# Where a routed feed-forward adds an expert's outputs back: at the end of its round, or after the second weight tile of the next round

## The reference

```python
def swiglu(h, wg, wu, wd):
    return (jax.nn.silu(h @ wg) * (h @ wu)) @ wd

def moe(h, router, wg, wu, wd):
    logits = (h @ router).astype(jnp.float32)
    vals, idx = lax.top_k(logits, TOP_K)
    w = jax.nn.softmax(vals, axis=-1)
    gates = jnp.sum(jax.nn.one_hot(idx, N_EXPERTS) * w[..., None], axis=-2)
    y = jnp.zeros_like(h)
    for e in range(N_EXPERTS):
        y = y + gates[..., e:e + 1] * swiglu(h, wg[e], wu[e], wd[e])
    return y
...
x = x + g2 * moe(h, ...)                           # D = 1024, D_FF = 3072
return rmsnorm(x, final_g)
```

## Time and profile before

| | us |
|---|---|
| median of three runs | 2789.95 |
| the profiled execution | 2787.62 |
| its span, first to last instruction | 2785.8 |
| PE busy in the span | 2625.9 |
| DVE busy | 1974.1 |
| ACT busy | 1384.5 |
| eight rounds of the routed feed-forward, about | 1889.7 to 2771.1 |

### The profile page before, as it was taken

One profiled execution on the slowest core, in us unless ns is written; L12 is line 12 of the kernel. 1 busy time (PEld: TensorE's weight loads), 2 busy tenths in 40 slices (PEclk: granted clock), 3 DMA queues, 4 the chain that ended last, 5 costly groups with the idle time before them and its releaser, 6 DMA issues. The chain is left out here.

```text
span 2785.8 us, 42232 instructions
## 1 busy us (share of the span) xinstructions
PE 2625.9 (94%) x14598; PEld 2260.7 (81%) x14598; DVE 1974.1 (71%) x2695; ACT 1384.5 (50%) x1697; POOL 0.2 (0%) x4
## 2 busy tenths in 40 slices
PE   8979878999999999999799998979999999999998
PEld 3769768887888889999687998867888888888886
DVE  6768235988777877776554653528788798898886
ACT  3454223133444444444353433427677777676775
POOL 0000000000000000000000000000000000000000
PEclk9999899999999999999999999989999999999999
DMA  6531223632678877876242553418899999998995
GB/s 243 210 114 46 69 76 123 190 112 90 226 264 291 298 281 257 282 257 228 90 166 77 182 183 123 167 61 304 321 364 333 326 373 330 358 347 322 371 333 210
DMA packets 223290, 626.83 MB, mean 225 GB/s; under 512 B 15296, under 2 KB 23520, under 8 KB 222816
## 3 DMA queue, kind: packets, MB, share of 16 engines
q1 hardware_dynamic: 223200, 625.64, 63.6%
HBM read 619.29 MB, written 6.29 MB: 225 GB/s over the span
## 5 line engine op out<-in xcount | busy, mean ns | idle before, releaser
L3133 DVE TENSOR_TENSOR wide_low<-wide,wide_high 128x2048 fp32r<-128x2048 f32 x288 | 657.1, 2286 | 125.9 <-ACT wide_high L3080 122.5
L3080 ACT ACTIVATE wide_high<-wide 128x2048 fp32r<-128x2048 f32 x288 | 550.9, 1918 | 182.7 <-DMA wide<-in_moe_gu 91.3
L229 DVE TENSOR_TENSOR expert_tile_low<-slot,expert_tile_high 128x1024 fp32r<-128x1024 f32 x216 | 263.9, 1223 | 129.9 <-ACT expert_tile_high L221 125.7
L221 ACT ACTIVATE expert_tile_high<-slot 128x1024 fp32r<-128x1024 f32 x216 | 227.3, 1054 | 189.2 <-PE bank L238 78.1
L2985 PE MATMUL bank<-wide_high,xg_high 128*128 128x512 f32 x768 | 305.4, 398 | 4.3 <-ACT wide_high L3080 4.3
L2986 PE MATMUL bank<-wide_high,xg_low 128*128 128x512 f32 x768 | 300.3, 391 | 0.0
L2989 PE MATMUL bank<-wide_low,xg_high 128*128 128x512 f32 x768 | 207.3, 392 | 0.2 <-DVE wide_low L3133 0.2
L237 PE MATMUL bank<-h_high,expert_tile_high 128*128 128x256 f32 x704 | 173.2, 284 | 0.0
L1899 PE MATMUL bank<-expert_tile_high,act_hi 128*128 128x512 f32 x512 | 161.3, 396 | 12.2 <-DVE act_lo L2040 12.2
L238 PE MATMUL bank<-h_low,expert_tile_high 128*128 128x256 f32 x704 | 172.7, 283 | 0.0
L2985 PEld LDWEIGHTS bank<-wide_high,xg_high 128*128 128x128 f32 x768 | 144.8, 189 | 33.6 <-ACT wide_high L3080 4.5
(11 more groups left out here) (500 smaller groups left out, 5084.1 us busy)
## 6 DMA issues: line engine op xcount, KB each, us to landing
wide<-in_moe_gu SPq DMA_DIRECT2D x192, 1024.0 KB, 5.8
wide<-in_moe_d SPq DMA_DIRECT2D x96, 1024.0 KB, 6.5
slot<-in_peer_u SPq DMA_DIRECT2D x128, 512.0 KB, 4.3
slot<-in_peer_v SPq DMA_DIRECT2D x128, 512.0 KB, 4.4
slot<-in_w_in SPq DMA_DIRECT2D x72, 512.0 KB, 3.4
picked_or_ada<-in_ada_w SPq DMA_DIRECT2D x48, 512.0 KB, 5.0
ada_slot<-in_ada_w SPq DMA_DIRECT2D x48, 512.0 KB, 4.6
slot<-in_ffn_gu SPq DMA_DIRECT2D x48, 512.0 KB, 3.4
```

The costliest lines, as they stand in the source:

```text
L221: core.nc.scalar.activation(self.tile_hi[:, place % 2], core.slot[u][:], ACT.Copy).then_inc(self.hi_ready.sem, 1)
L229: core.nc.vector.tensor_tensor(self.tile_lo[:, place % 2], slot[:], self.tile_hi[:, place % 2].bitcast(F32), ALU.subtract)\
L3080: nc.scalar.activation(w_hi[n % NB][:].rearrange("p c n -> p (c n)"), wide[n % U][:], ACT.Copy).then_inc(hi_ready.sem, 1)
L3133: nc.vector.tensor_tensor(w_lo[n % NB][:].rearrange("p c n -> p (c n)"), wide[n % U][:], w_hi[n % NB][:].rearrange("p c n -> p (c n)").bit ...
```

## The change

After the change the outputs are kept in banks 4 and 5 until the next round has begun. ACT copies them after its copy of tile 1, scaled by a column of shares for each place, to `y_high`; DVE makes `y_low` from the same bank behind the low part of tile 1. PE scatters behind tile 1: 16 matmuls, high and low part with `back`, which is now unscaled and F32R. The `take`s stand behind tiles 3 to 6, two each. `turn_pick` transposes `pick` with the identity and multiplies `pick` with a one-column vector of shares. The same round body now also scatters in the first round, where the banks, the column of shares and `back` are zero; after the loop one scatter follows for the last round.

```diff
-    yg = sb("yg", [P, D])
+    y_hi, y_lo = sb("y_high", [P, D], F32R), sb("y_low", [P, D], F32R)
-    back = sb("back", [P, N])
-    shared = sb("share_diagonal", [P, 2, P])
+    back = sb("back", [P, N], F32R)
+    of_tokens = sb("shares_of_tokens", [P, 2, 1])
+    of_places = sb("shares_of_places", [P, 1])
...
-    SPREAD = (6, 7, 1, 3)
+    SPREAD = (1, 3, 6, 7)
...
-            def scatter():
+            def scatter(k):
+                pe.wait_ge(backs.sem, backs.at(1) + k)
+                pe.wait_ge(x_ready.sem, x_ready.at(2) + k * 2)
                 for s in range(4):
+                    if s % 2 == 0:
+                        pe.wait_ge(y_split.sem, y_split.at(s // 2 + 1) + k * 2)
                     for j in range(2):
                         m = 2 * s + j
-                        last = nc.tensor.matmul(core.bank[SPREAD[s]][:, j * N:j * N + N], yg[:, m * P:m * P + P], back[:, :], start=True, stop=True)
+                        out = core.bank[SPREAD[s]][:, j * N:j * N + N]
+                        nc.tensor.matmul(out, y_hi[:, m * P:m * P + P], back[:, :], start=True, stop=False)
+                        last = nc.tensor.matmul(out, y_lo[:, m * P:m * P + P], back[:, :], start=False, stop=True)
                     last.then_inc(scattered.sem, 1)
...
             def turn_pick(k):
-                pe.wait_ge(diagonals.sem, diagonals.at(1) + k)
+                pe.wait_ge(columns.sem, columns.at(1) + k)
+                pe.wait_ge(y_split.sem, y_split.at(2) + k * 2)
                 for tt in range(2):
-                    last = nc.tensor.matmul(core.bank[4][:, tt * P:tt * P + P], pick[:, tt, :], shared[:, tt, :], start=True, stop=True)
+                    nc.tensor.transpose(core.bank[4][:, tt * P:tt * P + P], pick[:, tt, :], core.ident)
+                for tt in range(2):
+                    last = nc.tensor.matmul(core.bank[4][:, N:N + 1], pick[:, tt, :], of_tokens[:, tt, :], start=(tt == 0), stop=(tt == 1))
...
+                        if j == 0 and w == 0:
+                            scatter(k)
...
-                pe.wait_ge(backs.sem, backs.at(1) + k)
-                pe.wait_ge(y_kept.sem, y_kept.at(2) + k * 2)
-                pe.wait_ge(x_ready.sem, x_ready.at(4) + k * 2)
-                scatter()
+            scatter(n_rounds(pe))
...
+            def keep_outputs(k):
+                for b in range(2):
+                    if b == 0:
+                        act.wait_ge(y_made.sem, y_made.at(1) + k)
+                    else:
+                        act.wait_ge(used.sem, used.at(NB) + k * T)
+                    nc.scalar.activation(y_hi[:, 512 * b:512 * b + 512], core.bank[Y[b]][:, :], ACT.Copy, scale=of_places[:, 0:1])\
+                        .then_inc(y_kept.sem, 1)
...
+                    if n == 1:
+                        keep_outputs(k)
...
-                for b in range(2):
-                    act.wait_ge(y_made.sem, y_made.at(1) + k) if b == 0 else act.wait_ge(used.sem, used.at(NB + T) + k * T)
-                    nc.scalar.activation(yg[:, 512 * b:512 * b + 512], core.bank[Y[b]][:, :], ACT.Copy).then_inc(y_kept.sem, 1)
+            keep_outputs(n_rounds(act))
...
+            def low_outputs(k, b):
+                dve.wait_ge(y_kept.sem, y_kept.at(b + 1) + k * 2)
+                nc.vector.scalar_tensor_tensor(y_lo[:, 512 * b:512 * b + 512], core.bank[Y[b]][:, :], of_places[:, 0:1],
+                                               y_hi[:, 512 * b:512 * b + 512].bitcast(F32), ALU.mult, ALU.subtract).then_inc(y_split.sem, 1)
...
-                    if n < C:
-                        take(k, (4, 5, 6, 7, 0, 1, 2, 3)[n])
+                    if n == 1:
+                        for b in range(2):
+                            low_outputs(k, b)
+                    if 3 <= n < 7:
+                        for m in range(2 * n - 6, 2 * n - 4):
+                            take(k, m)
                     if n == C:
                         dve.wait_ge(pick_turned.sem, pick_turned.at(1) + k)
+                        nc.vector.tensor_copy(of_places[:], core.bank[4][:, N:N + 1])
                         nc.vector.tensor_copy(back[:, :], core.bank[4][:, 0:N]).then_inc(backs.sem, 1)
```

More of the change, by code:

```diff
@@ L2937, in routed_feed_forward @@
         "moe_silu", "moe_hidden", "moe_hidden_turned", "moe_hidden_high", "moe_hidden_low"))
-    picks, gathered, x_high, x_ready, backs, y_made, y_kept, scattered, added, diagonals, pick_turned = (core.count(n) for n in (
+    picks, gathered, x_high, x_ready, backs, y_made, y_kept, y_split, scattered, added, columns, pick_turned = (core.count(n) for n in (
         "picks_ready", "tokens_gathered", "gathered_high", "gathered_low", "backs_ready", "outputs_made", "outputs_kept",
-        "outputs_scattered", "outputs_added", "share_diagonals", "picks_turned"))
+        "outputs_low", "outputs_scattered", "outputs_added", "share_columns", "picks_turned"))
     J = D_FF // 512
@@ L3100, in make_pick, with take_shares @@
                 ins.then_inc(picks.sem, 1)
-            def make_diagonal(k):
+            def take_shares(k):
                 e = expert_of(dve, k)
-                for tt in range(2):
-                    ins = nc.vector.tensor_scalar(shared[:, tt, :], core.ident, shares[:, tt, bass.ds(e, 1)], None, ALU.mult)
-                ins.then_inc(diagonals.sem, 1)
+                nc.vector.tensor_copy(of_tokens[:], shares[:, :, bass.ds(e, 1)]).then_inc(columns.sem, 1)
+            def low_outputs(k, b):
+                dve.wait_ge(y_kept.sem, y_kept.at(b + 1) + k * 2)
+                nc.vector.scalar_tensor_tensor(y_lo[:, 512 * b:512 * b + 512], core.bank[Y[b]][:, :], of_places[:, 0:1],
+                                               y_hi[:, 512 * b:512 * b + 512].bitcast(F32), ALU.mult, ALU.subtract).then_inc(y_split.sem, 1)
             def low_gathered(k):
@@ L3121, in _ @@
             make_pick(0)
-            for b in (1, 3):
-                nc.vector.memset(core.bank[b][:, :], 0.0).then_inc(scattered.sem, 1)
-            make_diagonal(0)
+            nc.vector.memset(of_places[:], 0.0)
+            nc.vector.memset(core.bank[Y[1]][:, :], 0.0)
+            nc.vector.memset(core.bank[Y[0]][:, :], 0.0).then_inc(y_made.sem, 1)
+            for tt in range(2):
+                ins = nc.vector.tensor_copy(back[:, tt * P:tt * P + P], core.zeros[:].bitcast(F32))
+            ins.then_inc(backs.sem, 1)
+            take_shares(0)
             low_gathered(0)
-            for b in (6, 7):
-                dve.wait_ge(x_ready.sem, x_ready.at(2))
-                nc.vector.memset(core.bank[b][:, :], 0.0).then_inc(scattered.sem, 1)
             with dve.Fori(0, n_rounds(dve)) as k:
@@ L3134, in _ @@
                                             w_hi[n % NB][:].rearrange("p c n -> p (c n)").bitcast(F32), ALU.subtract).then_inc(lo_ready.sem, 1)
-                    if n < C:
-                        take(k, (4, 5, 6, 7, 0, 1, 2, 3)[n])
+                    if n == 1:
[4 more added lines that the diff above has]
+                            take(k, m)
                     if n == C:
                         dve.wait_ge(pick_turned.sem, pick_turned.at(1) + k)
+                        nc.vector.tensor_copy(of_places[:], core.bank[4][:, N:N + 1])
                         nc.vector.tensor_copy(back[:, :], core.bank[4][:, 0:N]).then_inc(backs.sem, 1)
                         make_pick(k + 1)
-                        make_diagonal(k + 1)
+                        take_shares(k + 1)
                     if n >= 5 and n % 4 == 1 and n < T1 + 4:
@@ L3154, in _ @@
             rounds = n_rounds(dve)
+            for b in range(2):
+                low_outputs(rounds, b)
             for m in range(C):
```

## The result

The changed kernel took 2774.09 us (median of five runs, 2771.97 to 2779.14) against 2789.62 for the kernel before (five runs): ratio 0.9941, 95% interval 0.9925 to 0.9956. Faster by 15.5 us; forecast were 14.3 us and 2775.6 us. In a second set of runs the same kernel had 0.9931 (0.9916 to 0.9947).

What follows compares the result with a forecast made beforehand. PE was taken to bound the kernel, with the weight loads near their limit. Seven turns gain 16.2 us, round 0 loses 2.3, the tail gains 0.4: 14.3 us off 2789.95 gives 2775.6 us, range 2770 to 2788.

Steps and rivals of the forecast that it cites:

- What bounds: Whole round: PE and weight loads both near their limit; PE waits only where a round ends.
- the 361 GB/s of mid-round: Load supply after the turn: at this rate a round needs 104.6 us, 2.8 less than PE's 107.4.
- The turn: PE between rounds: gap, old scatter and low-part wait go, new scatter and `turn_pick` come; net 2.3 us, seven turns 16.2.
- its slow first matmul: Tile 0's first matmul at the old turn, 0.41 us; left in place, cause unknown between scatter and loop's turn.
- the 0.08 us booked behind the new scatter: PE after the scatter: first wide matmul after small ones takes 0.31 us instead of 0.23.
- The bare turn: Rival at the round's end: loop's turn, no longer hidden behind the scatter, costs PE 3.37 us; 2799 to 2800 us; chance 0.05.
- ACT's order as cover: ACT at the turn: tiles 0 and 1 copied before the outputs, ready at -2.2 and -0.3 us from tile 0's start.
- Round 0 and the tail: First round scatters zeros, 2.3 us lost; after the last round copies and `take`s end earlier, 0.4 us gained.
- The room of `y_low`: DVE early in the round: both halves ready at 3.7 us, PE asks at 5.4; 1.7 us of room, 1.2 at worst.
- the rival of the late outputs: Rival: late tile 0 load brings output parts after 5.4 us; PE waits, 2 us a round gives 2789 us; chance 0.09.

Runs made afterwards that it cites:

- scatter_twice: Changed kernel with each pair of scatter matmuls issued twice, 32 instead of 16; a round took 108.97 us against 107.05.
- eleven_products: Changed kernel with one of the twelve matmuls of each tile left out; a round took 103.09 us against 107.05.
- plain_new_place: Changed kernel with the scatter behind tile 1 in plain 32-bit floats, without low part; round 108.57 us, ratio to the kernel before 0.9964.
- keep_first: Changed kernel with ACT's copies of the outputs ahead of its copy of tile 0 again; round 111.16 us, ratio to the kernel before 1.0042.
- split_old_place: Changed kernel with copies, low parts and F32R scatter at the end of the round; round 111.06 us, ratio to the kernel before 1.0033.
- no_zero_scatter: Changed kernel with first round written out without scatter, copies and adds, and 20 matmuls behind the last scatter; ratio to the kernel before 0.9945.
- after_tile_0: Changed kernel with the scatter behind tile 0 on PE instead of tile 1; a round took 107.44 us against 107.05.

## Why the prediction was right

- **What bounds.** PE, with the loads close behind. scatter_twice shows the first, eleven_products the second: room for 4.0 us a round, where the prediction had worked out 2.8 from the 361 GB/s of mid-round. That working was not sound. In that stretch PE was busy for 95.00 of 95.00 us, and a round of the kernel before without its turn takes PE about 104.9 us (109.69 - 4.43 - 0.38, the last two as below), which asks for 360 GB/s: the 361 was PE's own pace. What the loads could do lay only a little above it, 366 GB/s, which no row of before could show. That the conclusion held is in part luck.
- **The turn.** Forecast 4.63 us removed and 2.31 added, net 2.3. Measured 109.81 - 107.05 = 2.76 in the mean, 109.69 - 107.05 = 2.64 against the rounds of before that had no late load. The 4.43 us from tile 35 to tile 0 went whole, as forecast. The scatter was sized right (1.92, the row of the same form). Tile 0 took 3.10 us before and 2.72 now, 0.38 less, where only 0.2 was booked: the 0.18 us of its slow first matmul, left in place by the prediction, came from the plain scatter ahead of it and not from the loop's turn (plain_new_place has it behind tile 1). `turn_pick` grew by 0.22, not 0.31, and the 0.08 us booked behind the new scatter did not come: a wide matmul starts 0.23 after its predecessor there. That gives 4.43 + 0.38 - 1.92 - 0.22 = 2.67, near the 2.64.
- **The bare turn.** The loop's turn itself costs PE nothing: 2220.50 follows 2219.60 + 0.90, and this rival falls. The fetch after a taken branch to code outside the window, of which the Trainium skill speaks in "Runtime: NRT & Kernel Launch", section "Instruction fetch mechanics", is not to be seen. The instruction queues moved five packets each from 1880 to 2785 us; before it was five and four. The spacing that the Trainium skill gives in "TensorE: Matmul & The Clock Gate", section "Wait — 56ns, not 53.3ns?", would have made the scatter 1.75 us by an estimate; the new one took the 1.92 of the row.
- **Which part pays.** The prediction summed PE's terms and treated ACT's order as cover. The runs show that this cover is the condition: keep_first costs 4.1 us a round, split_old_place 4.0. The place gives 1.24, the form 1.52 on top of it; at the old place the form, with its extra step on VectorE, costs 1.25 (111.06 against 109.81).
- **Round 0 and the tail.** From the first gathered copy to the start of tile 35 of round 0 passed 111.08 us before and 113.40 now: 2.3 us lost, as forecast. From the last tile to the norm the gain was 0.4 us, as forecast: the last four matmuls started at 2764.51 before the norm at 2771.42 and now at 2754.83 before 2761.31, so 6.91 became 6.48.
- **What the sum had left out.** The stage gained 17.3 us: seven turns at 2.64, 0.7 from the late loads in two rounds of before, less 2.3 for round 0, and 0.4 at the end. The forecast was 14.3. The norm behind the stage took 1.7 us longer, since part of its matmuls ran at the lower clock; the prediction had no term for that. Stage and norm make 15.6, and the medians differ by 15.5. This near agreement isn't shown to be more than chance: the two profiled executions differ by only 8.5 us, since in the changed kernel's the stage began 7.2 us later. The prediction's closeness is partly luck as well, a turn sized 0.3 too small against a norm that took longer.
- **The room of `y_low`.** Forecast ready 3.7 us after tile 0's start, measured 2223.61 - 2220.50 = 3.1 us, PE asking at 5.4 as forecast. A half took 0.74 us, between the bounds of 0.68 and 0.95. With late loads the room of 2.3 us shrank to 0.15, so the rival of the late outputs came close without costing anything.

## What to carry to other kernels

Where an in-order engine copies results at the end of a round and then prepares the next round's first operands, put the preparation first, and move the consumer of the results behind enough work to cover the copy, the split and one late load. Then size the move by the engine that bounds: its own instructions in and out, read from rows of the same form, and ask how close the next chain is before believing any larger gain. A rate read in a stretch in which the bounding engine never waits is that engine's demand and not what the loads can do. A dose on each engine (twice the scatter, four more copies, one product less) answered in three runs what the waits view could only suggest.

## What the runs showed of the hardware

TensorE's clock before the closing norm. The granted clock was 0.72 from 2761 to 2767 us in the changed kernel, so part of the norm's 16 matmuls ran at 1.2 GHz and part at 2.4:

```profile
2761.78 5.41 PE L364 MATMUL bank<-sq_end,avg 128*128 128x256 f32 x16 [2.61 <-ACT sq_end L389]
```

and with the fill in no_zero_scatter:

```profile
2748.91 3.72 PE L364 MATMUL bank<-sq_end,avg 128*128 128x256 f32 x16 [0.75 <-ACT sq_end L389]
```

The new tail has an idle of 1.1 us before the scatter (for `y_low`) and of 2.6 after it. Of seven profiled executions with exactly this tail (six kernels) the 16 matmuls took 5.1 to 6.7 us in five and 3.72 in two (keep_first, eleven_products); with 1.69 us of idle ahead of them (before, plain_new_place, scatter_twice) or 0.75 (the filled tail, twice) they took 3.72 in all five. So the shorter scatter can cost up to 3 us where the longer one had kept TensorE busy.

The same shows in mid-stage. In keep_first PE was idle for 2.70 us at each of seven turns; the granted clock fell behind four of them, which cost some 1.0 us each, and not behind the other three. Idle times of 1.11 us at the seven turns of split_old_place and of 1.25 and 1.57 in after_tile_0 had no fall behind them. Why the clock falls after some idle times of 2.6 to 2.7 us and not after others is open.

The time ahead of the stage varies by itself. The first copy of gathered tokens began between 1881.1 and 1891.1 us in twelve profiled executions, though the work ahead of it is the same in all ten kernels. That is as large as most effects here, and is a reason why totals of one run can't rank these kernels, while the distance between scatters, where no load is late, agrees to hundredths.
